# DeltaNet heads of a hybrid decoder: TensorE's loop over the heads written out as straight code

## The reference

```
qkv   = silu(causal_short_conv(h[q,k,v]))          # h = rmsnorm(x) @ w_in
q, k  = l2norm(q) * DK**-0.5, l2norm(k)
# per chunk of tokens, state S (DK x DV):
decay = exp(G_i - G_j) (lower triangle);  G = cumsum(log_a)
lmat  = strict(beta * (k k^T) * decay)
u     = solve(I + lmat, beta * (v - exp(G) * (k S)))
o     = exp(G) * (q S) + ((q k^T) * decay) u
S     = exp(G_last) * S + (k * tail)^T u
out   = rmsnorm(o) * silu(z)                        # z also from h
```

## Time and profile before

| what | us |
|---|---|
| median of three runs | 3727.59 |
| the profiled execution, its own time | 3723.92 |
| its span, first to last instruction | 3722.3 |
| TensorE busy in it | 3519.4 (95%) |
| VectorE, ScalarE, GpSimd busy | 2019.9, 958.2, 1554.2 |

### The profile page before, as it was taken

One profiled execution on the slowest core, in us unless ns is written; L12 is line 12 of the kernel. 1 busy time (PEld: TensorE's weight loads), 2 busy tenths in 40 slices (PEclk: granted clock), 3 DMA queues, 4 the chain that ended last, 5 costly groups with the idle time before them and its releaser, 6 DMA issues. The chain is left out here.

```text
span 3722.3 us, 59489 instructions
## 1 busy us (share of the span) xinstructions
PE 3519.4 (95%) x23050; PEld 2657.4 (71%) x23050; DVE 2019.9 (54%) x3254; ACT 958.2 (26%) x2183; POOL 1554.2 (42%) x1575
## 2 busy tenths in 40 slices
PE   8999999997899999999999889899989999999999
PEld 5666666565678888788778656666668788887887
DVE  4454444443765555666622245555555655556666
ACT  3443444433111111100001035555531111111002
POOL 0101000012449999644221124444414499996432
PEclk9999999997999999999999999999989999999999
DMA  4111111102521211443322300000043212214422
GB/s 155 41 43 48 42 36 42 48 25 79 155 88 58 70 64 58 143 156 92 104 73 54 93 27 10 1 1 2 1 131 88 88 59 73 69 64 129 156 79 87
DMA packets 307956, 263.69 MB, mean 71 GB/s; under 512 B 30650, under 2 KB 283699, under 8 KB 305779
## 3 DMA queue, kind: packets, MB, share of 16 engines
q1 hardware_dynamic: 301988, 252.97, 22.2%
q0 software_dynamic: 2048, 5.25, 0.5%
q10 hardware_dynamic: 3650, 1.64, 0.2%
HBM read 212.81 MB, written 51.08 MB: 71 GB/s over the span
## 5 line engine op out<-in xcount | busy, mean ns | idle before, releaser
L1818 PE MATMUL ps<-xn,work 128*128 128x363 f32 (+1 forms) x1536 | 548.9, 487 | 15.8 <-issue 15.7
L405 PE MATMUL ps<-work 128*128 128x272 f32 x1612 | 384.4, 394 | 16.9 <-PEq L1640 7.3
L1818 PEld LDWEIGHTS ps<-xn,work 128*128 128x128 f32 x1536 | 272.0, 194 | 136.5 <-issue 30.4
L972 PE MATMUL ps<-work 128*128 128x272 f32 x1360 | 367.1, 392 | 0.0
L405 PEld LDWEIGHTS ps<-work 128*128 128x128 f32 x1612 | 306.6, 191 | 84.2 <-issue 21.0
L972 PE MATMUL ps<-xT,work 128*128 128x272 f32 x1280 | 340.6, 394 | 9.5 <-POOL work L1275 9.5
L972 PE MATMUL ps<-xn,work 128*128 128x272 f32 x1280 | 319.8, 392 | 0.0
L3572 POOL TENSOR_SCALAR work<-work 128x640 f32<-128x640 f32 (+7 forms) x256 | 198.4, 784 | 286.9 <-DVE work L3482 286.8
L972 PEld LDWEIGHTS ps<-work 128*128 128x128 f32 x1360 | 258.4, 190 | 53.3
L704 POOL TENSOR_TENSOR xT<-xT,work 128x272 f32<-128x272 f32 x96 | 195.4, 2048 | 227.4 <-DVE work L555 143.6
L972 PEld LDWEIGHTS ps<-xT,work 128*128 128x128 f32 x1280 | 241.7, 190 | 66.0 <-POOL work L1275 17.2
(11 more groups left out here) (504 smaller groups left out, 6026.9 us busy)
## 6 DMA issues: line engine op xcount, KB each, us to landing
work<-in_ffn_w_in_dram SPq DMA_DIRECT2D x160, 256.0 KB, 3.2
xn<-in_ffn_w_out_dram SPq DMA_DIRECT2D x46, 704.0 KB, 4.7
work<-in_gdn_w_in_dram SPq DMA_DIRECT2D x32, 512.0 KB, 4.1
work<-in_ffn_w_out_dram SPq DMA_DIRECT2D x18, 704.0 KB, 4.6
work<-in_gdn_w_out_dram SPq DMA_DIRECT2D x44, 256.0 KB, 3.4
ffn_parked_hidden_late<-work SPq DMA_DIRECT2D x20, 544.0 KB, 2.9
work<-ffn_parked_hidden_late SPq DMA_DIRECT2D x2, 5440.0 KB, 24.0
ffn_parked_residual<-xT SPq DMA_DIRECT2D x2, 4352.0 KB, 12.8
```

The source lines that it names most:

```text
L405: mm = pe.matmul(acc(n, a), w[:, k, :], t[:, k, :], start=(first and k == 0), stop=(k == hk - 1), skip_group_check=True)
L972: ins = pe.matmul(acc(a, n), w[:, k, :], t[:, k, :], start=(first and k == 0), stop=(k == 1), skip_group_check=True)
L1818: mm = pe.matmul(unit_acc(u, m), w[j % 2][:, k, :], c.xn[:, k, o:o + cnt], start=(k == 0), stop=(k == KD - 1))
```

## The change

Only TensorE's program changes. The loop over the first seven heads becomes a loop of the program that builds the kernel, so the body of `head` is put out eight times with `i` a constant. The order of the products, the waits and the values that they compare with stay what they were.

```diff
@@ -2087,9 +2087,8 @@
                 for _ in first:
                     pass
                 pe.wait_ge(z, 5)
-                with pe.Fori(0, HG - 1) as i:
-                    head(i, True)
-                head(HG - 1, False)
+                for i in range(HG):
+                    head(i, i < HG - 1)
```

## The result

The changed kernel took 3685.95 us in the median of four runs (3677.84 to 3693.80), the kernel before 3728.22 us in four (3724.97 to 3732.45). The ratio is 0.9901, 95% interval 0.9876 to 0.9925. The forecast was 3697 us, a gain of 30.5 us; the range began at 3682.

What follows compares the result with a forecast made beforehand. TensorE, busy for 95% of the span, was taken to bound the kernel. Gains of 15.7 + 10.7 + 4.1 = 30.5 us took 3723.9 to 3693.4 us; 3.7 us for the runs' median gave 3697 us, range 3682 to 3713.

Steps and rivals of the forecast that it cites:

- The six jumps, idle time: Between DeltaNet heads, TensorE's idle time at six taken loop jumps goes: 15.7 us of gain.
- it doesn't do what it says: Rival: at the seam the next packet isn't there in straight code either; 3723 us, chance 0.04.
- The half clock behind each jump: In the first fill after each jump, half clock costs 1.78 us more; removing six gains 10.7 us.
- the dips stay: Rival: six clock dips turn up behind other small waits, so that gain is 0; 3708 us, chance 0.12.
- What is late next at the seam: Between heads, ACT and DVE don't hold PE up after the jump goes: 0, at most 2.4 us lost.
- Register work: PE's computing of looped wait values hides behind its queue: 0, at most 11 us of gain.
- Fetching inside the body: Ahead of L1950, fetches race gate-row transfers; 8 of 12.1 us remain, bounds 12.1 us gain to 8.9 us loss.
- term 3: The gain from fewer fetch stalls and dips ahead of L1950 in the looped heads: 4.1 us.
- slower rival: Rival: all seven heads lose the gate-row race in full, 42 us in place of 12.1; 3731 us, chance 0.03.
- The last head: Four waits ahead of L1969, 3.9 us; code unchanged, only packet edges move: 0, bounds 3.9 us either way.
- no fetch stalls in straight code: Rival: the 8 us left and the last head's 3.9 us go too; 3685 us, chance 0.13.
- term 2: The gain from losing the half clock in the fill behind each of six jumps: 10.7 us.

Runs made afterwards that it cites:

- hidden jump: Against the kernel before: loop kept for heads 0 to 5, head 6 straight, jump placed behind the next head's first fill; 3694.94 us, ratio 0.9922.
- three experiments that keep such an idle time: Loop with gate rows loaded later (3709.22 us), straight code with a 2.9 us wait at each seam (3718.28 us), heads 0 to 3 looped (3697.12 us).
- looped kernel with late gate rows: Kernel before, loop kept, with SP loading the next head's gate rows some 27 us later; 3709.22 us, ratio 0.9969.
- 224 no-operations: Changed kernel with 224 PE no-operations put ahead of the first head, meant to move packet edges; 3688.10 us, ratio 0.9920 to the kernel before.
- loop of four: Against the kernel before: heads 0 to 3 in the loop, 4 to 7 straight, three jumps instead of six; 3697.12 us, ratio 0.9931.
- one-trip loops: Against the kernel before: each of heads 0 to 6 in its own loop that runs once, no branch taken; 3683.59 us, ratio 0.9893.

## Why the prediction was right, point by point

**The six jumps, idle time (15.7 us).** Right. No wait is left at the seams, half of the jumps cost half, and a hidden jump costs nothing though its branch is nearly as long. Of the rivals, "it doesn't do what it says" is out.

**The half clock behind each jump (10.7 us).** Right for this pair of profiles; as a rule too large. An undisturbed head went from 103.14 to 98.5 us, 4.6 us for the 4.5 forecast. But I took the six dips of six in the profile of before as certain, and the looped kernel with late gate rows has them at three of six nearly equal seams. A jump that nothing hides cost 2.5 to 2.9 us of idle time each time, and 1.8 us more often, not always. Over the three experiments that keep such an idle time, 8 of 15 seams had the dip. The rival "the dips stay" has its mechanism half right: dips do follow other idle times, and the clock behind nearly equal idle times differs from seam to seam.

**What is late next at the seam (0).** Right. PE waits for no engine there. ACT's root ends 5.7 us behind the end of L1941, as before, and DVE's scaling 8.6 us behind it, as before, though the fill now starts at once.

**Register work (0).** Right, by the looped head of 98.53 us with its jump hidden.

**Fetching inside the body (12.1 us, 8 left).** The size came out in the first profile, and by luck: head 0 of after is 5.5 us longer than before's against its start (1.8 us earlier, end 3.7 us later), and head 1 2.0 us, so 7.5 us are left, as stalls in two heads and a dip of 3.0 us and not in three heads as guessed. In the second profile two stalls of 4.8 us together are left and no dip, in the third one of 1.3 us. On average some 4.5 us are left and not 8, so term 3 was too small by 3 to 4 us. The prediction also held that the fetching is only moved; with two packets fewer for each jump (8 in a straight head, 10 in a looped one) there is less of it. That the transfers of the gate rows cause the stalls in these heads was argued from one burst and is now shown. The slower rival, all seven hit, is out: of seven heads at most two stalled in any profile of the unchanged straight code.

**The last head (0, with bounds of 3.9 us either way).** This is the term that was most wrong. Its code did not change, yet its four "issue" waits of 3.9 us are gone in all three profiles of the straight code, and four such waits (3.5 us) are there again in the looped kernel with late gate rows. From the L1941 at its start to the one at its end it took 89.06 us before and 85.36, 85.46 and 84.38 in the three profiles of the straight code: 3.6 to 4.7 us of gain. Why is open. It was not a race with another transfer: from 862 to 880 us, where all four waits stand, before has only instruction packets on the DMA engines.

```profile
q8 instruction: 3, 0.05, 1.1%
```

It does not come with every loop either: with four or six heads looped this stretch took 84.8 and 84.1 us. The rival "no fetch stalls in straight code", 3685 us, is right here and not in head 0, and lies nearest to the measured median. The page of the Trainium skill that it leaned on (Runtime: NRT & Kernel Launch, Instruction fetch mechanics: crossing a block's edge in sequence is mostly hidden) holds in every head that takes 98.5 us. It fails where another transfer fills the DMA engines. In the last head of before, where none does, there are waits on "issue" too, and no run here shows whether they are fetches.

**From 30 to 42 us.** The heads up to the L1941 of head 6 give 839.43 - 805.04 = 34.4 us, the last head 3.7 more. Of these 38 us, 8 are given back outside the change, so that 30.1 show. For these stretches I give windows of before, then of after: the last recurrence with the output projection, from 35.5 us ahead of the last L1941 on, and the start of the sparse layer, where PE has the same wait of 2.75 us in both.

```profile
893.00:960.00 67.00, 53.46 (x277) 41.54 (x277) 26.32 (x50) 19.34 (x40) 14.11 (x15) 0.92 0.50 158
...
1840.00:1885.00 45.00, 41.91 (x138) 23.16 (x137) 25.73 (x19) 2.90 (x4) 19.09 (x8) 1.00 0.65 238
```

```profile
854.92:921.92 67.00, 54.68 (x260) 41.53 (x260) 23.84 (x45) 19.31 (x40) 12.40 (x12) 0.84 0.51 157
...
1805.00:1850.00 45.00, 39.92 (x121) 22.33 (x120) 28.76 (x19) 2.42 (x3) 19.86 (x8) 0.92 0.65 238
```

The granted clock is 0.92 against 0.84, and 1.00 against 0.92. The code of these stretches is the same, and the second of them is at 1.00 again in the profile with 224 no-operations and at 0.85 in the second one of the straight code. From the last L1941 to the end of the span it is 2793.8 us before and 2801.7, 2805.3 and 2801.6 in the three profiles of the straight code, but 2794 to 2804 with no-operations or late gate rows, which change nothing there. Thus the profiled execution of after was an unlucky one and that of before most likely a lucky one, which the medians even out: 4.3 us on the one side, 7.9 on the other, and 30.1 becomes 42.3. Beside each other the medians of before and after differ by 42.3 us in the result and by 27.8 and 32.5 us in the two repeats, with ratios of 0.9901, 0.9917 and 0.9911. All 51 runs of before have a median of 3721.2 us, all fourteen of the straight code 3687.1, 34 us apart. The gain is some 30 to 40 us, nearer to the forecast of 30.5 than the first 42. The four runs of before in the result (median 3728.2) stand above the medians of its other three sets (3718.7 to 3723.6), those of after do not stand apart. Whether that is luck or the chip can't be settled by these runs. The terms as the runs leave them give an estimate: 15.7 us of idle time, 7.1 of half clock (14 of 21 seams of four profiles, 6 x 1.78 x 2/3), 7.6 of fetching in the heads (12.1 less the 4.5 left) and 4 in the last head, 34.4 us together. Against the forecast, term 2 was put too large and the other two too small, and in part the errors made up for each other.

## What to carry to other kernels

Before unrolling a loop, look at the sequencer's row of the branch: its spread between the fall-through (83 ns here) and the taken jumps (4.3 us) is the price before anything hides it, and only what the engine's queue does not cover of it is lost (2.5 to 2.9 us of idle time here, often with a slower clock behind it). The loop can be kept if the jump is placed behind a group of long instructions. A wait on "issue" in the middle of dense small products may be a fetch that lost a race: look at whether a transfer fills the DMA engines there, and move that one. If none does, as in the last head here, this does not explain it. And look into the trace of an experiment for what it was to keep: the one-trip loops had lost their register work.

## What the runs showed of the hardware that I had not expected

Equal idle times of TensorE did not always lead to the same clock. Behind 2.5 to 2.9 us of idle time at a seam the granted clock was 0.50 at six of six seams before, at three of six in the looped kernel with late gate rows, at four of six with a wait in place of the jump, and at one of three in the loop of four. Behind 0.7 us it stayed at 1.00 at six of six. A single profile says little on how often such a price is paid.

Each taken jump of PE's loop also brought two more instruction packets than straight code: 197, 195 and 191 of them with six, five and three jumps, 185 with none.
